# Transposes of mixer outputs and queries: VectorE's 32x32 blocks and DMA in place of TensorE

## What is computed

```
def hybrid_layer(x, ...):
    h = rmsnorm(x, pre_g)
    pr = split_columns(h @ w_in)      # the inputs of four mixers (4936 columns) and four gates (8192)
    ya = gmlp_branch(pr['a_u'], pr['a_v'], ...) * silu(pr['a_z'])
    yb = mla_branch(pr['b_cq'], pr['b_ckv'], pr['b_kr'], ...) * silu(pr['b_z'])
    yc = dsa_branch(pr['c_q'], pr['c_k'], pr['c_v'], pr['c_iq'], ...) * silu(pr['c_z'])
    yd = swa_sink_branch(pr['d_q'], pr['d_k'], pr['d_v'], ...) * silu(pr['d_z'])
    merged = sum(sigmoid(gate[b]) * (y[b] @ w_branch[b]) for b in range(4))
    return x + rmsnorm(merged @ w_out, post_g)
```

## Time and profile before

| | us |
|---|---|
| profiled execution, its own time | 1721.39 |
| its span, first to last instruction | 1719.6 |
| TensorE matmul busy | 1697.5 (99%) |
| VectorE busy | 1035.0 (60%) |
| ACT busy | 777.0 (45%) |
| GpSimd busy | 182.3 (11%) |
| loads on SP's queue, share of 16 DMA engines | 60.3% |

### The profile page before, as it was taken

The page is one execution under the profiler, slowest core; times in us unless marked ns, Lnnn a source line. Parts: engine busy times, 40 slices in busy tenths (PEclk is TensorE's granted clock), DMA queues, the critical chain, the costliest instruction groups (busy, mean ns, idle before and its releaser), DMA issues.

```text
span 1719.6 us, 19969 instructions
## 1 busy us (share of the span) xinstructions
PE 1697.5 (99%) x7926; PEld 1410.2 (82%) x7926; DVE 1035.0 (60%) x1298; ACT 777.0 (45%) x996; POOL 182.3 (11%) x221
## 2 busy tenths in 40 slices
PE   8999999999999999999999999999999999999997
PEld 6888888887888888888788888888788888888886
DVE  6468556666555555555474695655765655554654
ACT  6444444443444444444364434444444444444442
POOL 1020127400000000000010211193000000000000
PEclk9999999999999999999999999999999999999999
DMA  9765575555555766666576655656456556666663
GB/s 321 207 191 179 166 211 158 171 160 184 174 177 150 228 193 192 196 209 207 151 251 195 189 177 176 196 155 176 147 184 194 172 169 208 197 189 193 211 212 113
DMA packets 167261, 323.58 MB, mean 188 GB/s; under 512 B 10304, under 2 KB 62272, under 8 KB 166912
## 3 DMA queue, kind: packets, MB, share of 16 engines
q1 hardware_dynamic: 165152, 315.53, 60.3%
q0 software_dynamic: 1728, 6.50, 1.3%
q10 hardware_dynamic: 288, 0.28, 0.0%
HBM read 318.07 MB, written 4.19 MB: 187 GB/s over the span
## 4 chain that ended last, share of the span: by engine, by line
PE 91%; DVE 5%; DMA 1%; ACT 1%; issue 1%; DVEq 0%; SPq 0%; ACTq 0%
PE ps L1359 29%; PE ps L1361 29%; PE ps L1360 29%; PE ps L1375 3%; DVE w_lo L818 2%; DMA raw<-in_w_in_dram 1%; PE ps L1409 1%; ACT w_hi L494 1%; PE ps L1432 1%; DVE proj L1191 1%; DVE proj L1175 0%; DVE top L1189 0%; ACT area L517 0%; PE ps L1445 0%; DVE wide L924 0%
## 5 line engine op out<-in xcount | busy, mean ns | idle before, releaser
L818 DVE TENSOR_TENSOR w_lo<-raw,w_hi 128x1024 fp32r<-128x1024 f32 (+2 forms) x590 | 733.4, 1253 | 621.5 <-ACT w_hi L494 620.4
L494 ACT ACTIVATE w_hi<-raw 128x1024 fp32r<-128x1024 f32 (+2 forms) x591 | 615.3, 1048 | 823.0 <-PE ps L1361 782.2
L1359 PE MATMUL ps<-w_hi,lhs 128*128 128x512 f32 (+1 forms) x2036 | 796.5, 391 | 6.9 <-DVE w_lo L818 6.9
L1360 PE MATMUL ps<-w_lo,lhs 128*128 128x512 f32 (+1 forms) x2036 | 790.3, 388 | 0.0
L1361 PE MATMUL ps<-w_hi,lhs 128*128 128x512 f32 (+1 forms) x2036 | 790.3, 388 | 0.0
L1359 PEld LDWEIGHTS ps<-w_hi,lhs 128*128 128x128 f32 x2036 | 382.5, 188 | 88.4 <-DVE w_lo L818 7.1
L1361 PEld LDWEIGHTS ps<-w_hi,lhs 128*128 128x128 f32 x2036 | 382.5, 188 | 77.6
L1360 PEld LDWEIGHTS ps<-w_lo,lhs 128*128 128x128 f32 x2036 | 382.8, 188 | 75.0
L1359 PE MATMUL ps<-w_hi,yT 128*128 128x512 f32 (+1 forms) x304 | 116.7, 384 | 0.0
L1361 PE MATMUL ps<-w_hi,yT 128*128 128x512 f32 (+1 forms) x304 | 116.6, 383 | 0.0
L1360 PE MATMUL ps<-w_lo,yT 128*128 128x512 f32 (+1 forms) x304 | 116.5, 383 | 0.0
(11 more groups left out here) (181 smaller groups left out, 742.3 us busy)
## 6 DMA issues: line engine op xcount, KB each, us to landing
raw<-in_w_in_dram SPq DMA_DIRECT2D x256, 512.0 KB, 4.3
raw<-in_w_in_dram SPq DMA_DIRECT2D x191, 502.0 KB, 4.4
raw<-in_w_branch_dram SPq DMA_DIRECT2D x64, 512.0 KB, 3.7
raw<-in_w_out_dram SPq DMA_DIRECT2D x64, 512.0 KB, 4.4
raw<-in_b_w_uq_dram SPq DMA_DIRECT2D x8, 384.0 KB, 3.3
wide<-in_x_dram SPq DMA_DIRECT2D x2, 1024.0 KB, 8.4
raw<-in_b_w_ukv_dram SPq DMA_DIRECT2D x8, 256.0 KB, 2.7
proj<-in_post_norm_g_dram POOLq DMA_DIRECT2D x2, 1024.0 KB, 5.8
```

What stands on the lines that cost most here:

```text
L494: act.activation(wslot(w_hi, s, n), wslot(raw, s, n), ACT.Copy).then_inc(hi_done, 1)
L818: dve.tensor_tensor(wslot(w_lo, s, n), wslot(raw, s, n), wslot(w_hi, s, n).bitcast(F32), ALU.subtract).then_inc(lo_done, 1)
L1359: pe.matmul(o, hi, wh[:, k], start=a, stop=False)
L1360: pe.matmul(o, hi, wl[:, k], start=False, stop=False)
```

## The change

Five transposing steps leave TensorE (`yA`, `yB`, `yC`, `C1`, `D1`), except for the small turns of `c_k` and `c_ik` in step `C2`. In their place VectorE transposes each 32x32 block within its band of 32 partitions (`blocks_turned`) into a part of `area`, which is free at that time, and SP moves the blocks to their bands with DMAs (`move`): band a of the source goes in four DMAs to the four bands of the destination, in pieces of 32 floats. For each array this is done for a = 0 to 3, each time ahead of one weight load. The outputs of A, B and C are then read from `area` by ACT (`moved_hi`) and VectorE (`y_turned`) and split into halves as before; B and C later than before, in G 1 and G 6. Queries and D's keys are moved straight to their places in `turned`. The diff, cut to its core:

```diff
+        def in_rows(ap):
+            return ap.rearrange("p (i c) -> p i c", c=NW)
+        yA_blocks, yA_turned = in_rows(area[:, 0, 0:1024]), in_rows(area[:, 1, 0:1024])
...
+        d_blocks, d_turned = in_rows(area[:, 0, 0:1024]), in_rows(rows(0, 4).rearrange("p k s -> p (k s)"))
+        dk_blocks, dk_turned = in_rows(area[:, 0, 1024:1536]), in_rows(rows(4, 2).rearrange("p k s -> p (k s)"))
+        cq_blocks, cq_turned = in_rows(area[:, 0, 1024:2048]), in_rows(rows(0, 4).rearrange("p k s -> p (k s)"))
+        ciq_blocks, ciq_turned = in_rows(area[:, 1, 0:1024]), in_rows(rows(7, 4).rearrange("p k s -> p (k s)"))
@@ SP
+            def move(dst, src, a, moved):
+                p = slice(32 * a, 32 * (a + 1))
+                blocks = src[p].rearrange("p i (kt b s) -> p i kt b s", b=4, s=32)
+                for b in range(4):
+                    to = dst[32 * b:32 * (b + 1)].rearrange("p i (kt a s) -> p i kt a s", a=4, s=32)
+                    sp.dma_start(to[:, :, :, a], blocks[:, :, :, b]).then_inc(moved, 16)
+            def moves(l, j):
+                if 7 * CPG + 9 <= j < 7 * CPG + 9 + 4:
+                    sp.wait_ge(dve_s.sem, dve_s.at(l, "yAt"))
+                    move(yA_turned, yA_blocks, j - (7 * CPG + 9), yA_moved)
...              (yB at GATE0 + 9, yC at GATE0 + 5 * CG + 9)
+                if GATE0 + 5 * CG + 5 <= j < GATE0 + 5 * CG + 5 + 4:
+                    sp.wait_ge(dve_s.sem, dve_s.at(l, "dt"))
+                    move(d_turned, d_blocks, j - (GATE0 + 5 * CG + 5), d_moved)
+                    move(dk_turned, dk_blocks, j - (GATE0 + 5 * CG + 5), d_moved)
+                if GATE0 + CG + 9 <= j < GATE0 + CG + 9 + 4:
+                    sp.wait_ge(dve_s.sem, dve_s.at(l, "ct"))
+                    move(cq_turned, cq_blocks, j - (GATE0 + CG + 9), c_moved)
+                    move(ciq_turned, ciq_blocks, j - (GATE0 + CG + 9), c_moved)
             def load(l, j, slot, src):
                 if l > 0 or j >= SLOTS:
                     sp.wait_ge(lo_done, l * CHUNKS + j + 1)
+                moves(l, j)
@@ ACT
+            def moved_hi(l, name, moved, src, buf, scale):
+                act.wait_ge(moved, l * 256 + 256)
+                for i in range(2):
+                    last = act.activation(yT[:, buf, 0, 2 * i:2 * i + 2].rearrange("p k s -> p (k s)"), src[:, i], ACT.Copy, scale=scale)
+                last.then_inc(*act_s.did(name))
...
-                    if G == 1:
-                        act.wait_ge(pe_s.sem, pe_s.at(l, "C1"))
-                        evac(cqT[:, 0:2].rearrange("p k s -> p (k s)"), 4)
-                        evac(ciqT[:, 0:2].rearrange("p k s -> p (k s)"), 6).then_inc(*act_s.did("C1"))
@@ VectorE
+            def blocks_turned(dst, src):
+                for t in range(TT):
+                    to = dst.rearrange("p i (k t c) -> p t i k c", t=TT, c=P)[:, t]
+                    last = dve.transpose(to, src[:, t].rearrange("p (i k c) -> p i k c", k=2, c=P))
+                return last
...                  (group 7, after A2)
+                dve.wait_ge(dve_s.sem, dve_s.at(l, "A2"))
+                blocks_turned(yA_blocks, u).then_inc(*dve_s.did("yAt"))
...                  (after the first split of G)
+                    if G == 5:
+                        dve.wait_ge(pool_s.sem, pool_s.at(l, "d"))
+                        blocks_turned(d_blocks, part("d_q", BW))
+                        blocks_turned(dk_blocks, dk_twice).then_inc(*dve_s.did("dt"))
...                  (after the fifth split of G)
+                    if G == 0: (after B6)
+                        blocks_turned(yB_blocks, part("b_cq", BW)).then_inc(*dve_s.did("yBt"))
                     if G == 1:
-                        dve.wait_ge(pe_s.sem, pe_s.at(l, "C1"))
-                        dve.tensor_copy(cqT[:, 2:4].rearrange("p k s -> p (k s)"), bank(5))
-                        dve.tensor_copy(ciqT[:, 2:4].rearrange("p k s -> p (k s)"), bank(7)).then_inc(*dve_s.did("C1"))
+                        dve.wait_ge(pool_s.sem, pool_s.at(l, "c"))
+                        blocks_turned(cq_blocks, part("c_q", BW))
+                        blocks_turned(ciq_blocks, part("c_iq", BW)).then_inc(*dve_s.did("ct"))
...                  (G 5: the same for yC after C7; G 6: D1's two copies go)
@@ TensorE
-                    if g == 9:
-                        turn_y("yA", part("a_u", BW))
...                  (turn_y of yB and yC, C1 and D1 go in the same way)
                     if G == 2:
                         seen(act_s, "C2")
+                        pe.wait_ge(c_moved, l * 512 + 512)
                     if G == 6: (after its fifth chunk)
+                        pe.wait_ge(d_moved, l * 512 + 512)
```

More of the change, by code:

```diff
@@ L76 @@
 GELU_C, GELU_S = 0.044715, float(np.sqrt(2.0 / np.pi))
[L79 to L83, removed]
+PE_STEPS = (["A2", "B1", "B3k", "B3q", "B4", "B5", "B6",
+             "C2", "C3", "C4", "C5", "C6", "C7",
+             "D2", "D4", "D6a", "D3", "D5", "D6b", "M0", "M1", "M2", "out3"])
+ACT_STEPS = (["ss", "gelu", "zA", "B1", "zB", "yA", "B3k", "B3q", "B4", "zC", "B5", "zD",
+              "yB", "C2", "C3", "C4", "C5", "C6", "yC", "D2", "D4", "zT0", "D3", "D5", "zT1", "yD",
               "M0", "M1", "M2"] + [f"sq{n}{t}" for n in range(4) for t in range(2)])
-DVE_STEPS = (["rn", "A1", "gelu", "vn", "zA", "Bn", "A2", "B1", "yA", "zB", "B3k", "ikn", "B3q", "B4max",
-              "B5", "B6", "zC", "yB", "zD", "C1", "C3", "sel0", "C4", "sel1", "C5max", "C6", "C7", "yC",
-              "D1", "D2max", "zr0", "D4", "D6a", "D3max", "zr1", "D5", "D6b", "yD", "M0", "M1", "M2"] +
+DVE_STEPS = (["rn", "A1", "gelu", "vn", "zA", "Bn", "A2", "yAt", "B1", "yA", "zB", "B3k", "ikn", "B3q", "B4max",
+              "B5", "B6", "yBt", "zC", "zD", "ct", "yB", "C3", "sel0", "C4", "sel1", "C5max", "C6", "dt", "C7", "yCt",
+              "yC", "D2max", "zr0", "D4", "D6a", "D3max", "zr1", "D5", "D6b", "yD", "M0", "M1", "M2"] +
              [f"og{n}" for n in range(3)])
@@ L171, in trunk @@
         x_loaded = [sem(f"x_loaded{i}") for i in range(2)]
+        yA_moved = sem("yA_moved")
+        yB_moved = sem("yB_moved")
+        yC_moved = sem("yC_moved")
+        d_moved = sem("d_moved")
+        c_moved = sem("c_moved")
         first_x, first_loaded, first_hi, warm = sem("first_x"), sem("first_loaded"), sem("first_hi"), sem("warm")
@@ L258, in load_residual @@
             eng.dma_start(area[:, :, c], src[0].rearrange("(t p) d -> p t d", p=P)[:, :, c]).then_inc(res_loaded[n], 16)
+        def in_rows(ap):
+            return ap.rearrange("p (i c) -> p i c", c=NW)
+        yA_blocks, yA_turned = in_rows(area[:, 0, 0:1024]), in_rows(area[:, 1, 0:1024])
+        yB_blocks, yB_turned = in_rows(area[:, 0, 0:1024]), in_rows(area[:, 1, 1024:2048])
+        yC_blocks, yC_turned = in_rows(area[:, 1, 0:1024]), in_rows(area[:, 1, 1024:2048])
+        d_blocks, d_turned = in_rows(area[:, 0, 0:1024]), in_rows(rows(0, 4).rearrange("p k s -> p (k s)"))
+        dk_blocks, dk_turned = in_rows(area[:, 0, 1024:1536]), in_rows(rows(4, 2).rearrange("p k s -> p (k s)"))
+        cq_blocks, cq_turned = in_rows(area[:, 0, 1024:2048]), in_rows(rows(0, 4).rearrange("p k s -> p (k s)"))
+        ciq_blocks, ciq_turned = in_rows(area[:, 1, 0:1024]), in_rows(rows(7, 4).rearrange("p k s -> p (k s)"))
         block = ctx.enter_context(nc.Block())
@@ L264, in _ @@
         def _(sp):
+            def move(dst, src, a, moved):
[8 more added lines that the diff above has]
+                    move(yA_turned, yA_blocks, j - (7 * CPG + 9), yA_moved)
+                if GATE0 + 9 <= j < GATE0 + 9 + 4:
+                    sp.wait_ge(dve_s.sem, dve_s.at(l, "yBt"))
+                    move(yB_turned, yB_blocks, j - (GATE0 + 9), yB_moved)
+                if GATE0 + 5 * CG + 9 <= j < GATE0 + 5 * CG + 9 + 4:
+                    sp.wait_ge(dve_s.sem, dve_s.at(l, "yCt"))
+                    move(yC_turned, yC_blocks, j - (GATE0 + 5 * CG + 9), yC_moved)
+                if GATE0 + 5 * CG + 5 <= j < GATE0 + 5 * CG + 5 + 4:
[6 more added lines that the diff above has]
+                    move(ciq_turned, ciq_blocks, j - (GATE0 + CG + 9), c_moved)
             def load(l, j, slot, src):
@@ L643, in _ @@
                 splits(l, j + 4, j + 5)
-                for i in range(2):
-                    turned_hi(l, "yA", 4 + i, yT[:, 0, 0, 2 * i:2 * i + 2].rearrange("p k s -> p (k s)"), 0.125, last=(i == 1))
+                moved_hi(l, "yA", yA_moved, yA_turned, 0, 0.125)
                 splits(l, j + 5, j + 8)
@@ L706, in _ @@
                         softmax(1, C_HEADS, c_place, 512, C_DIM ** -0.5).then_inc(*act_s.did("C5"))
-                    if G == 6:
-                        act.wait_ge(pe_s.sem, pe_s.at(l, "D1"))
-                        evac(dqT[:, 0:2].rearrange("p k s -> p (k s)"), 4).then_inc(*act_s.did("D1"))
                     if G == 7:
@@ L730, in _ @@
                         last.then_inc(*act_s.did("yD"))
[L731 to L734, removed]
```

(32 more changed lines are left out.)

1 line of the change is left out of this document (added).

## The result

The changed kernel takes 1751.07 us (median of four runs, 1750.0 to 1752.5) against 1720.9: ratio 1.0173, 95% interval 1.0156 to 1.0189, slower by 1.7% or 30 us. The forecast was 1711.1, with a range up to 1726. The profiled execution has a span of 1749.4 us, 29.8 more than before.

A forecast was written before the change was run, and what follows sets the result against it. TensorE's matmuls were taken to bound the kernel. From 1721.4 us, 11.3 came off for removed blocks and 2 x 0.5 was added for waits at the index scores: 1711.1 us, own range 1709 to 1714, full range 1707 to 1726.

The forecast's parts named there:

- What one costs SP: SP's queue: issuing a move takes 0.45 us and a load 0.4, with ends of 0.37 and 0.6.
- a new wait of 0 to 1 us; I put 0.5 per layer: Index scores: c's moves land at 356 to 357.5 us, TensorE wants them at 357.32; 0.5 us wait per layer.
- first step: TensorE's stream: each microsecond removed comes off the time, as long as what feeds it keeps its lead.
- 3.9 us to spare: Fourth load among d's moves: issued at 462.3 us, split by 469.1, 3.9 us before TensorE takes it.
- Behind it come mixer C's steps: After d's moves: mixer C's steps take 2.2 us on SP and 3.0 on the engines; lag is worked off later.
- Rival 1: SP's queue: moves take 0.6 us each, costing 5.4 us per layer; 1721 us, no change; chance 0.17.
- Rival 3: DMA engines: a 128-byte piece is as dear as one of 1 KB, 46 ns; 1748 us, slower; chance 0.15.
- The blocks, 11.3 us: TensorE: removed blocks save 0.87 us each for mixers A, B, C, 1.75 for C1, 1.31 for D1; 5.67 per layer.
- The two halves of y are read from SBUF in place of PSUM, in the same number: ACT and VectorE: reading mixer outputs from SBUF leaves the number of half reads unchanged; no cost was counted.
- The transposes: VectorE: 14 new transposes per layer, taken at 0.7 us by the 128x512 copy.
- rival 2: VectorE: transposes cost twice the price taken, delaying c's moves by 2.4 us; 1716 us; chance 0.12.
- The clock: TensorE: at its full 2.4 GHz before; a fall in it would show the prediction wrong.

The follow-up runs named there:

- number 8: Kernel before, plus groups of four DMAs of various forms behind its last store; issue took 0.61 us for the move's form from SBUF, 0.45 from HBM.
- number 10: Whole change except c_q and c_iq, which stay TensorE's; mixer outputs, d_q and D's keys are moved: 1735.38 us, ratio 1.0084 to the kernel before.
- number 6: Whole change plus 16 idle matmuls on TensorE ahead of its wait for c's moves: 1751.11 us, ratio 1.0175 to the kernel before.
- Number 4: Whole change, with c_q and c_iq moved together and d_q with D's keys, same bytes and pieces: 1714.42 us, ratio 0.9958 to the kernel before.
- number 7: Whole change, unmerged, with GpSimd issuing all moves in place of SP: 1735.92 us, ratio 1.0082 to the kernel before.

## Why the prediction was wrong, by its steps

**What failed: "What one costs SP".** "A move has a load's form ... I take 0.45 for a move and 0.4 for a load, the two ends 0.37 and ... 0.6". Measured: 0.65 from one move to the next, above my upper end, and 0.7 for the load behind them. I went by the shape of the rows and missed that all of the earlier trace rows read from HBM (number 8). The kernel before has stores from SBUF to HBM, at 0.33 to 0.39 us to issue, but no DMA with both ends in SBUF; that was the thing to say, and no bound from loads could then close the range.

**c, "a new wait of 0 to 1 us; I put 0.5 per layer".** It is 7.2. By my own formula with measured terms: the moves start at 336.76, not 338.8; 3 x 5.9 + 5.2 us later, at 359.7, the last is out, and at 361.2 it has landed. TensorE came not at 357.32 but at 354.2, since the blocks of A, B and C1 were gone from ahead of it. That second mistake is 3 us: I took the time at which TensorE wants c from the trace of before, though my own first step had moved it. What a change frees ahead of a wait that it adds is to be added to that wait.

**d, "3.9 us to spare".** The step is 5.9 us, not 4.0; the fourth load went out 24.1 us after the first move (476.37 - 452.26), with one move of 1.95 us in it, where I had 15.6. The wait is 3.3 us at the load, and more behind it.

**"Behind it come mixer C's steps ... the lag stays and is worked off later."** I counted 2.2 us on SP for one. They take 3.3, over a chunk's 2.72, so that the lag grows: 9.7 us in both layers (number 10), half of what SP's price cost at c.

**Rival 1** named the cause, with 0.17 and a time of 1721. It was 30 us short: 0.05 us more a move and 0.3 more a load are 2.5 us at c; the rest is in what is told above of TensorE's earlier time, of d and of the moves behind it. My range ended below it.

**Rival 3** came within 3 us of the time, for a reason that is not there. In one microsecond of the kernel after in which only moves run, its DMA queue:

```profile
q1 hardware_dynamic: 526, 0.06, 39.0%
```

39.0% of 16 us over 526 pieces: 11.9 ns each, less than the 20 I took. The agreement of a total proves no cause. Three groups of number 8 move the same 128 KB: as moves within SBUF (4.0 us of trace), as moves from HBM (3.4 us), and within SBUF in pieces of 1 KB (3.7 us). Their DMA queue:

```profile
q1 hardware_dynamic: 1088, 0.13, 20.2%
...
q1 hardware_dynamic: 1088, 0.13, 25.1%
...
q1 hardware_dynamic: 192, 0.13, 13.7%
```

The share times 16 engines times the stretch is 12.9, 13.7 and 8.1 us of engine time: a piece of 128 bytes costs 11.9 ns within SBUF and 12.6 from HBM, where one of 1 KB, counted with its semaphores as in the earlier trace rows, costs 42. So the small piece is far from as dear as the large one, which was rival 3, but the same bytes are 1.6 times as dear in small pieces, within SBUF too. The Trainium skill's "Why small descriptors are slow" in "DMA: Bandwidth & Descriptors" says that transfers within SBUF are spared the penalty of small pieces. These groups do not bear that out, though my forecast named it in its favour. Nor do they show what I read into the Trainium skill's rule on less than 512 bytes, in the Specifications of "DMA: Bandwidth & Descriptors": a piece as dear as a far larger one.

**The blocks, 11.3 us.** Right for B and C (0.88 of 0.87), nearly for C1 (1.67 of 1.75) and D1 (1.23 + 0.14 of 1.31), wrong for A (0.14): 4.9 per layer, and 4.3 with the 0.6 to 0.7 lost at G 7. "The two halves of y are read from SBUF in place of PSUM, in the same number": in number, but in another place of the list, ahead of D's softmax. The outputs alone were worth 1.6 us by the medians, 2.5 by their blocks less that loss, not 5.2.

**The transposes** cost what I took, 0.69 us; rival 2 is out. The kernel after:

```profile
L916 DVE STREAM_TRANSPOSE area<-proj 128x512 f32<-128x512 f32 x24 | 15.4, 686 | 0.2
```

**The clock** I named only as a sign of being wrong. It fell behind each long wait. By number 6 that was 0.4 us at c in layer 0: there slow matmuls took the place of waits for loads that were late anyway. For the other waits no run tells it apart.

What held is the first step: a block that leaves TensorE's stream is a gain as long as what feeds it keeps its lead. Number 4, with half the DMAs for queries and keys, is at -6.2 us (-9.5 to -5.2 by its interval), where the worth of the five blocks less the loss at G 7 is 2 x 4.3 = 8.6.

## What to carry to other kernels

Price the issue of a DMA by a row with the same source and destination memories, not by one of the same shape; where no row has them, take an upper end well over the nearest and ask what the queue behind it does. Moves that share a queue with loads are to be few and large, here four per load and not eight: compare one step of the queue with the time in which the consumer uses one load. And move the consumer's own time forward by what the change frees ahead of it before you compare.

## What the runs showed of the hardware

- A DMA of 16 to 64 KB on SP's queue with both ends in SBUF took 0.53 to 0.73 us to issue, with 32 pieces or 512 (number 8); the moves' form from HBM took 0.33 to 0.45, a store from SBUF to HBM 0.33 to 0.39. GpSimd needed 0.57 us for a move (number 7).
- A piece of 128 bytes took a DMA engine 11.9 ns within SBUF and 12.6 from HBM (number 8).
- A load from HBM behind moves took 0.60 us to issue, a lone one 0.37.
- VectorE's transposes of 32x32 blocks, 128x512 float32, took 0.69 us, as its copies of that size do.
